# Low halves of weights on VectorE in the first layer, and the adaptive tiles moved to other stages

## The reference, cut to what matters

```
# first network, layer i (0: fox, 1: retention)
h = rmsnorm(x, norm_g[i]); proj = h @ w_in[i]
main = fox_attention(q, k, v, f) or retention(q, k, v)
memo = mem_cross_attention(q_mem, mem_n, w_mem_kv[i])
x = x + (concat(main, memo) * silu(z)) @ w_out[i]
# second network
mod   = silu(c)     @ w_ada + b_ada      # 1024 -> 6 * 1024
mod_c = silu(c_ctx) @ w_ada + b_ada      # only its first 2 * 1024 are used
h_lat = rms_norm(x, norm_mix) * (1 + sc1) + sh1
```

## Time and profile before

| | |
|---|---|
| median of 3 runs | 1732.31 us (1730.98 to 1733.33) |
| the profiled execution | 1731.86 us, its span 1729.9 us |
| TensorE busy | 1658.5 us, 96% of the span |
| VectorE, ScalarE, GpSimd busy | 806.7, 665.0 and 673.7 us |
| mean granted TensorE clock | 0.985 of full speed |

### The profile page before, as it was taken

The page is one execution under the profiler, slowest core; times in us unless marked ns, Lnnn a source line. Parts: engine busy times, 40 slices in busy tenths (PEclk is TensorE's granted clock), DMA queues, the critical chain, the costliest instruction groups (busy, mean ns, idle before and its releaser), DMA issues.

```text
span 1729.9 us, 19937 instructions
## 1 busy us (share of the span) xinstructions
PE 1658.5 (96%) x8222; PEld 1356.9 (78%) x8222; DVE 806.7 (47%) x1123; ACT 665.0 (38%) x978; POOL 673.7 (39%) x315
## 2 busy tenths in 40 slices
PE   8889999999999999999999999989989899999997
PEld 7777888788878778888877757678878688888885
DVE  6786766575655344443443645752352411111113
ACT  8422333333323433444444453135534443232322
POOL 0453334333334334334334315433303365464642
PEclk9999999999999999999999999999999899999999
DMA  6254242424245323232232222112101222222221
GB/s 242 105 170 147 92 153 86 153 85 153 107 156 187 110 85 98 98 98 98 97 102 86 85 86 97 49 73 77 49 1 50 73 98 97 98 97 98 97 86 49
DMA packets 52387, 176.01 MB, mean 102 GB/s; under 512 B 6332, under 2 KB 6972, under 8 KB 51912
## 3 DMA queue, kind: packets, MB, share of 16 engines
q1 hardware_dynamic: 52296, 174.73, 29.2%
HBM read 169.44 MB, written 2.12 MB: 99 GB/s over the span
## 4 chain that ended last, share of the span: by engine, by line
PE 83%; DVE 11%; ACT 3%; issue 1%; POOL 1%; DMA 0%; DVEq 0%; SPq 0%; ACTq 0%
PE banks L77 83%; DVE ada L77 2%; DVE Sc L77 1%; DVE T L77 1%; DVE TM L77 1%; ACT L77 1%; DVE X L77 1%; ACT T L77 0%; ACT R L77 0%; POOL wl L77 0%; DVE mx L77 0%; ACT Sc L77 0%; DVE Y L77 0%; DVE HL L77 0%; DVE QG L77 0%
## 5 line engine op out<-in xcount | busy, mean ns | idle before, releaser
L77 POOL TENSOR_TENSOR wl<-raw,wh 128x1024 fp32r<-128x1024 f32 x237 | 586.1, 2480 | 719.1 <-ACT wh L77 719.1
L77 PE MATMUL banks<-HH,wh 128*128 128x512 f32 x1040 | 416.8, 401 | 13.0 <-ACT HH L77 11.4
L77 PE MATMUL banks<-HL,wh 128*128 128x512 f32 x1040 | 407.4, 393 | 0.7 <-DVE HL L77 0.7
L77 ACT ACTIVATE wh<-raw 128x1024 fp32r<-128x1024 f32 x246 | 258.2, 1055 | 381.3 <-PE banks L77 365.8
L77 PE MATMUL banks<-HH,wl 128*128 128x512 f32 x1040 | 284.1, 391 | 1.2 <-POOL wl L77 1.2
L77 PEld LDWEIGHTS banks<-HH,wh 128*128 128x128 f32 x1040 | 197.2, 190 | 60.6 <-ACT HH L77 12.2
L77 PEld LDWEIGHTS banks<-HL,wh 128*128 128x128 f32 x1040 | 196.9, 189 | 45.9 <-DVE HL L77 3.8
L77 PEld LDWEIGHTS banks<-HH,wl 128*128 128x128 f32 x1040 | 196.3, 189 | 42.7 <-POOL wl L77 1.6
L77 PE MATMUL banks<-wh,HH 128*128 128x256 f32 x448 | 128.3, 286 | 0.0
L77 PE MATMUL banks<-wl,HH 128*128 128x256 f32 x448 | 126.8, 283 | 0.0
L77 PE MATMUL banks<-wh,HL 128*128 128x256 f32 x448 | 126.7, 283 | 0.0
(11 more groups left out here) (289 smaller groups left out, 2529.5 us busy)
## 6 DMA issues: line engine op xcount, KB each, us to landing
raw<-wst_dram SPq DMA_DIRECT2D x294, 512.0 KB, 3.3
CB<-sums_dram SPq DMA_DIRECT2D x12, 256.0 KB, 3.0
D<-dec_dram SPq DMA_DIRECT2D x12, 256.0 KB, 2.9
X<-xT_dram SPq DMA_DIRECT2D x4, 512.0 KB, 5.8
out_dram<-X SPq DMA_DIRECT2D x8, 256.0 KB
QS<-QX SPq DMA_DIRECT2D x24, 64.0 KB, 2.6
KSw<-KX SPq DMA_DIRECT2D x24, 64.0 KB, 2.0
MX<-memT_dram SPq DMA_DIRECT2D x2, 512.0 KB, 9.1
```

The source lines that it names most:

```text
L77: i = w[0](*w[1], **w[2])
```

## The change

Four things change.

- The low half of a weight unit is made on VectorE up to unit 72, where before it was so up to unit 8. GpSimd makes it from unit 73 on.
- The plan has no adaptive tile in the memory stage. Groups 2 to 4 go into the fox periods, one tile for two units as before, group 5 into the first output projection, and the groups 0 and 1, whose tiles are used twice, into the first periods of retention, two tiles for two units, eight such groups of four instructions.
- There are seven accumulators in place of four, four of them in space that the attention outputs use later; the reduction of one is split in two halves that go to two different units.
- `fox_scores(11)` is written ahead of the last unit of z instead of behind it, and `even_norm(5)` behind the first unit of the second output projection instead of ahead of it.

```diff
-    left = list(range(47, -1, -1))
+    left = [8 * g + k for g in (2, 3, 4, 5, 0, 1) for k in range(8)][::-1]
...
-    for l, j in ((0, 2), (0, 3), (1, 0)):
-        kv(l, j)
-        ada(left.pop())
+    kv(0, 2)
+    kv(0, 3)
+    kv(1, 0)
...
             pair("out0", k, k + 4, (256 * n,))
-            if left:
+            if k % 8 == 0:
                 ada(left.pop())
...
     for p in range(6):
         for cols in ((128 * p, 768 + 128 * p), (1536 + 256 * p,), (3584 + 256 * p,)):
             pair("ret", 0, 8, cols)
+            for _ in range(2):
+                if left:
+                    ada(left.pop())
...
-        if u < 9:
+        if u < 73:
             m2 = tt(wl[:, q, :], raw[:, s, :], wh[:, q, :].bitcast(F32), ALU.subtract, after=[m1, *w_free[q]])
...
-        targets = [((0, 2, 0, 2, 2, 2)[g], small["sc"])] + ([((1, 3)[g], small["scc"])] if g < 2 else [])
-        while k == 0 and g > 3 and later:
+        targets = [((2, 4, 0, 6, 1, 1)[g], small["sc"])] + ([((3, 5)[g], small["scc"])] if g < 2 else [])
+        while k == 0 and g == 5 and later:
...
-        unit_f(HH, HL)
+        unit_f(HH, HL, beside=(lambda: fox_scores(11)) if p == 5 else None)
         for j in range(2):
             M["z", j] = gate_in(j, [M["z read"]], Zt[:, j, :], RX)
         fox_attend(2 * p)
-        fox_scores(2 * p + 1)
+        if p < 5:
+            fox_scores(2 * p + 1)
...
-    even_norm(5)
...
-    steps = {(0, 0): [lambda: ret_attend(11), lambda: ret_square(11)], (0, 1): [lambda: ret_rstd(11), lambda: ret_norm(11), load_fo], (3, 1): [filter_norm]}
+    steps = {(0, 0): [lambda: even_norm(5), lambda: ret_attend(11), lambda: ret_square(11)], (0, 1): [lambda: ret_rstd(11), lambda: ret_norm(11), load_fo], (3, 1): [filter_norm]}
```

More of the change, by code:

```diff
@@ L114, in weight_plan @@
     pair("fox", 0, 8, (5132 + 1536,))
-    for l, j in ((0, 2), (0, 3), (1, 0)):
-        kv(l, j)
-        ada(left.pop())
+    kv(0, 2)
+    kv(0, 3)
+    kv(1, 0)
     pair("fox", 0, 8, (4876,))
[L119 to L123, removed]
+    kv(1, 1)
+    kv(1, 2)
     pair("fox", 0, 8, (5132 + 1792,))
-    ada(left.pop())
-    ada(left.pop())
     kv(1, 3)
-    ada(left.pop())
     for p in range(6):
@@ L285, in build @@
     later = []
-    ada_acc = [at("ada%d" % i, [128, 1024], o) for i, o in enumerate((140, 144, 201.5, 104))]
-    ada_mark, ada_free = [None] * 4, [[], [], [], []]
+    ada_acc = [at("ada%d" % i, [128, 1024], o) for i, o in enumerate((140, 201.5, 100, 104, 108, 112, 144))]
+    ada_mark, ada_free = [None] * 7, [[] for _ in range(7)]
     silu_c = []
@@ L297, in load_raw, with ada_reduce @@
         landed[i] = sp.dma(SP.dma_start, raw[:, s, :], a["wst"][i], s_raw[s], after=raw_free[s])
-    def ada_reduce(which, dst, bias):
+    def ada_reduce(which, dst, bias, h):
         def go():
[L301 to L309, removed]
+            b = bank[6 + h if which in (0, 1, 6) else 6]
+            for j in range(4):
+                k = tr(b.ap[:, 128 * j:128 * j + 128], ada_acc[which][:, 512 * h + 128 * j:512 * h + 128 * j + 128],
+                       after=[ada_mark[which], *b.free], mark=(j == 3))
+            r = dve.do(V.tensor_reduce, dst[:, 4 * h:4 * h + 4],
+                       b.ap.rearrange("p (j q) -> p j q", j=4), AX.X, ALU.add, after=[k])
+            b.free = [r]
             ada_free[which] = [k]
-            ada_done.append(tt(dst, dst, bias, ALU.add, after=[r]))
+            if h:
+                ada_done.append(tt(dst, dst, bias, ALU.add, after=[r]))
         return go
@@ L328, in ada @@
         if k == 7:
[L329 to L332, removed]
+            for i, (w, _) in enumerate(targets):
+                d = (mod, modc)[i][:, 8 * g:8 * g + 8]
+                for h in range(2):
+                    later.append((st["take"] + 4 + 2 * i + h, ada_reduce(w, d, P("bada", 8 * g, 8), h)))
     def split_next():
@@ L929, in build @@
     M["pe"] = bank[1].done
+    for i in range(2, 6):
+        ada_free[i] = [M["pe"]]
     RS = at("RS", [128, T], C0 + 2)
```

## The result

| | before | changed |
|---|---|---|
| median of 20 runs on the same chip | 1733.2 us (1730.05 to 1736.57) | 1729.22 us (1724.94 to 1733.07) |
| ratio | | 0.9979 [0.9972, 0.9986] |
| the profiled execution | 1731.86 us, span 1729.9 | 1725.07 us, span 1723.0 |

The change is faster by 4.0 us (0.2%), clear of noise but a good deal less than the 10.5 us forecast. Over the 20 runs the time goes with the mean granted clock, 0.987 in this one and 0.982 in the run of 1731.49 us.

A forecast was written before the change was run, and what follows sets the result against it. TensorE, busy 1658.5 of 1729.9 us, was taken as the bound, leaving 71 us idle. Terms 14.3 + 7.1 + 0.7 + 3.0 + 0.7 - 15.3 = 10.5 us took 1731.9 to 1721.4 us; range 1709 to 1731.

The forecast's parts named there:

- What bounds the kernel, and the memory stage: TensorE's 71 us idle bounds the gain; of the memory stage's 17.1 us of waits, 14.3 won, plus 7.1 from clock.
- Fox periods: VectorE's 48 low halves there fit in what the stretching had cost; nothing lost, and the 0.7 us `Kt` wait may go.
- Two moved steps: Moving `fox_scores(11)` and `even_norm(5)` removes waits of 3.0 us for a softmax and 0.7 us for `SQ`.
- Retention, "15.3 lost": Eight groups of four adaptive instructions in retention's first three periods cost 13.6 us of waits plus 1.7 of lower clock.
- the 5.8: Retention, ahead of `keep`: waits of 2.0, 0.3 and 3.5 us in the first three periods, because groups exceed VectorE's spare time.
- the 4.8: Retention: delay from the group ahead of `R` runs into the next `keep`, 2.4 us in the second and third periods.
- the 1.4 at `Zt`: Retention, ahead of `Zt`: a group with GpSimd tiles and a low half makes TensorE wait 0.7 us, twice.
- the 1.6 at `PT`: Start of retention: the first group delays the memory head's `PT` by 1.6 us.
- The sum: Whole kernel: 14.3 + 7.1 + 0.7 + 3.0 + 0.7 - 15.3 = 10.5 us won.
- the 26 that I gave as the upper bound: Retention's loss in us if every group of adaptive instructions runs at the stretched rates.
- the signs that I had named for being wrong: TensorE waits in fox periods, memory stage keeps over 6 us of waits, or retention's waits under 6 or over 22.
- The slower rival: Retention: groups ahead of `keep` and `Zt` run stretched by GpSimd, 44.8 us lost against 25.8 won, 1751 us; chance 0.07.

The follow-up runs named there:

- the spread plan: Changed kernel with one twice-used adaptive tile for each two units from unit 90 on, in place of two from unit 98 on: 1707.95 us, 0.9856.

## Why the prediction was right or wrong

- *What bounds the kernel, and the memory stage:* right. 17.1 us of waits became 2.8, exactly where the prediction put them (unit 11, behind the running sum), all four falls of the clock went in the profiled execution, and the running sum took 1.22 us undisturbed, where I had taken 1.1. The fall that the prediction allowed for behind unit 11 (1.7 us) is absent there, but it came in six of the eight profiled kernels that have this wait. VectorE's load was forecast at 65 us and is 69.7.
- *Fox periods:* right. No wait for TensorE from 165 us to the end of the projection, the multiply-adds at 1.28 us in the fox periods, `Kt`'s wait gone. One sign was off: GpSimd's first low half came at 449.99 us, not after 480, and its second stretched head 11's scalings to 3.37 us, which cost no wait.
- *Two moved steps:* right, 3.0 and 0.7 us.
- *Retention, "15.3 lost":* this step failed, in its size and in part of its mechanism. Its sum had only the places ahead of `keep`, `Zt` and the memory head's `PT`. For `keep` it said 5.8 + 4.8; the trace has 2.89 + 0.87 with a third hidden, and the kernel without reductions, where nothing hides it, has 2.91 + 0.72 + 2.97 = 6.6. So the 5.8 was about right and the 4.8 did not come (the queue delay that I carried from one period into the next mostly did not arrive), nor did the 1.4 at `Zt` and the 1.6 at `PT`. What it left out is the bank: I counted the reduction's sum as 0.9 us of VectorE's time and never asked what stands still while it is queued. The reductions are 12.1 us of waits in the profile, 8.3 of them behind a group, and the kernel with the sums ahead of the tiles (7.2 us faster) and the one without reductions (14.3) show that it is real. The falls of the clock were under-counted as well: 1.7 us forecast, 4.3 in the profile (half of 3.40 + 5.11).
- *The sum:* in the profiled execution retention gave back 23.8 us between the landmarks, 20.6 without the 3.2 us of transposes that only moved, where 15.3 was forecast; the other side won 29.5 - 3.2 = 26.3 against 25.8. Between medians the double tiles cost 28.2 us (26.8 by the ratios), 25.0 (23.6) without the transposes: just under the 26 that I gave as the upper bound and the 25.8 from which the change would be no gain; the other side then won 27 to 28. The nearly 3 us between the profiled executions' difference of 6.8 and the 4.0 of the medians are how far these two executions lie from their medians. None of the signs that I had named for being wrong came: retention's waits sum to 16.1 us, inside my 6 to 22, but three quarters of it stand where I had looked for nothing.
- *The slower rival* had one part right and its size wrong: passes stretched to 3.4 us were there, but nine of the 28 multiply-adds in retention were stretched, for 17 us of VectorE's time in all, and none of those ahead of the first two `keep` places. (The prediction read the median of 1.67 us as "most met none"; 1.27 is the fastest, so that median is itself a stretched pass.) The Trainium skill ("SBUF — State Buffer", Who interferes with whom) says that such a pair excludes each other, the second waiting for the whole of the first. The trace agrees: in the change, GpSimd's two tiles around the group at 698.39 us took 6.72 us together (the row of GpSimd's timeline below) where two took 4.77 in the earlier trace rows, and the multiply-adds beside them 3.42 us each, 2.15 more than the 1.27 of one alone. With GpSimd's low halves out of retention the same group took 5.9 us, of which 1.0 (2.32 - 1.28) is still a stretch, beside GpSimd's `OL`.

```profile
700.79 6.72 POOL L77 TENSOR_TENSOR wl<-raw,wh 128x1024 fp32r<-128x1024 f32 x2
```

- *What I did not see at all:* the forecast treated the two halves of the change as one. It gave the credit for the memory stage to the tiles that left, and the low halves alone win 17 us, four times what both win together. The plan as it stood took that back; spread, it is worth having, 1707.95 us against the 1712.61 of the low halves and the moved steps without it.

What stays open: how much of the gap between profile sums and medians is the clock (where the falls lie is known of the profiled executions alone; other runs have lower mean clocks), and why removing 3 us of waits from the spread plan did not show in its median.

## What to carry to other kernels

Ask of each instruction that is put in a list not only what it delays, but what it holds: a sum behind a block of filler work keeps a PSUM bank, and the engine that waits for the bank belongs to a step that has nothing to do with either. Here filler work that was nearly hidden two instructions at a time was not hidden four in a row; spread it before you move it, and put releases ahead of filler in program order. And when a change has two parts that repair the same stage, run each alone: here one line alone won four times as much as the whole.

## What the runs showed of the hardware

- VectorE's multiply-add over two SBUF operands of 128 x 1024 float32 took 1.27 us alone and up to 3.46 us with GpSimd's pass over such a tile beside it; moving 64 of GpSimd's 2.49 us passes to VectorE, at 1.22 each and with nothing else changed, left VectorE busy for 17.4 us less than before (789.3 against 806.7).
- The running sum (`TENSOR_TENSOR_SCAN`, 128 x 512) took 1.22 us, against 0.68 for a subtraction of the same size.
- The wait of 2.8 us at unit 11 came with a fall of the granted clock in six of the eight profiled kernels that have it, and with none in two (the change and the spread plan). The window from 60 to 72 us, in the changed kernel, then in the one without double tiles, then in the one without reductions, all with the same instructions in this stage:

```profile
60.00:72.00 12.00, 9.34 (x70) 8.95 (x71) 7.69 (x8) 3.96 (x7) 0.00 (x0) 1.00 0.52 176
```

```profile
60.00:72.00 12.00, 9.09 (x60) 8.83 (x61) 6.77 (x7) 4.21 (x8) 0.00 (x0) 0.86 0.49 160
```

```profile
60.00:72.00 12.00, 9.43 (x56) 9.31 (x56) 5.88 (x6) 3.43 (x7) 0.00 (x0) 0.72 0.44 138
```

The granted clock there is 1.00, 0.86 and 0.72. The same wait therefore costs differently from one execution to another.
